# Moving ten of sixteen blocks of S5 angles and sines to the MLA head, and the other six into gate units 2 to 4

## The reference, cut to what matters

```
q_dn, kv_dn, k_rope, gate = jnp.split(h @ w_in, MLA_SPLITS, axis=-1)
q   = _rmsnorm(q_dn, q_norm) @ w_uq        # per head: 128 + 64
out = (v * jax.nn.silu(gate)) @ w_out
```

```
lam_dt  = lam * dt[:, None]
lam_bar = jnp.exp(lam_dt)
powers  = jnp.exp(lam_dt[None] * jnp.arange(1, S5_CHUNK + 1)[:, None, None])
xs      = associative_scan(combine, (a, bu)) + powers[None] * h[:, None]
```

## Time and profile before

| what | value |
|---|---|
| median of 3 runs | 1923.38 us (1921.63 to 1929.44) |
| the profiled execution, its own time | 1926.24 us |
| its span in the trace | 1924.3 us |
| mean granted TensorE clock | 0.945 |
| PE matmul busy | 1676.7 us, 87% |
| DVE, ACT, POOL busy | 635.7, 443.5 and 511.9 us |

### The profile page before, as it was taken

How to read it: one execution, slowest core, us unless ns; L and a number is a source line. 1 busy time by engine, 2 the same in 40 slices (tenths; PEclk the granted TensorE clock), 3 DMA queues, 4 the chain that set the end, 5 groups by cost and what they waited for, 6 DMA issues and landing times.

```text
span 1924.3 us, 27570 instructions
## 1 busy us (share of the span) xinstructions
PE 1676.7 (87%) x10824; PEld 1256.0 (65%) x10824; DVE 635.7 (33%) x1201; ACT 443.5 (23%) x986; POOL 511.9 (27%) x451
## 2 busy tenths in 40 slices
PE   3899599999999789996666679999989988999997
PEld 3444255555544478885555568888878876888886
DVE  4538655555610222305555510000122022233301
ACT  1413433332300110114445420000020101144300
POOL 0039999999999810000000000000000000000000
PEclk9999799999999889997888789999999999999999
DMA  8665525434544212264667644444334332344431
GB/s 268 183 186 197 213 77 166 153 131 140 174 149 164 109 44 66 88 231 149 210 210 218 194 147 153 153 153 153 131 109 131 120 100 88 110 153 153 148 121 60
DMA packets 225439, 283.69 MB, mean 147 GB/s; under 512 B 22498, under 2 KB 209477, under 8 KB 216901
## 3 DMA queue, kind: packets, MB, share of 16 engines
q1 hardware_dynamic: 214976, 231.78, 37.9%
q0 software_dynamic: 7040, 41.95, 6.2%
q10 hardware_dynamic: 3333, 8.71, 1.1%
HBM read 226.82 MB, written 47.19 MB: 142 GB/s over the span
## 4 chain that ended last, share of the span: by engine, by line
PE 72%; SPq 9%; DVE 8%; ACT 4%; DMA 3%; issue 3%; DVEq 0%; ACTq 0%; PEldq 0%
PE bank L814 34%; PE bank L1140 12%; SPq L640 9%; PE bank L1010 6%; PE bank L879 2%; DMA arena<-arena 2%; PE bank L838 2%; PE bank L1196 1%; PE bank L943 1%; PE bank L912 1%; PE bank L911 1%; PE bank L909 1%; PE bank L910 1%; PE bank L907 1%; ACT arena L1506 1%
## 5 line engine op out<-in xcount | busy, mean ns | idle before, releaser
L814 PE MATMUL bank<-ht,ring 128*128 128x256 f32 (+1 forms) x1664 | 421.9, 417 | 18.6 <-DVE ht L2113 9.0
L814 PEld LDWEIGHTS bank<-ht,ring 128*128 128x128 f32 x1664 | 319.6, 192 | 119.4 <-issue 80.6
L1140 PE MATMUL bank<-arena,ring 128*128 128x256 f32 x1024 | 222.8, 381 | 1.1 <-PEq L1131 1.1
L1140 PEld LDWEIGHTS bank<-arena,ring 128*128 128x128 f32 x1024 | 195.6, 191 | 28.0 <-issue 1.2
L814 PE MATMUL bank<-gate,ring 128*128 128x256 f32 (+1 forms) x640 | 194.8, 467 | 4.5 <-DVE gate L2166 3.4
L814 PEld LDWEIGHTS bank<-gate,ring 128*128 128x128 f32 x640 | 122.4, 192 | 76.5 <-issue 62.7
L1010 PE MATMUL bank<-ring,ht 128*128 128x256 f32 x512 | 113.6, 384 | 12.1 <-DVE ht L1783 12.1
L1010 PEld LDWEIGHTS bank<-ring,ht 128*128 128x128 f32 x512 | 98.2, 193 | 26.1 <-issue 12.7
L814 PE MATMUL bank<-arena,ring 128*128 128x256 f32 x480 | 107.8, 388 | 3.9 <-DVE arena L2228 3.9
L814 PEld LDWEIGHTS bank<-arena,ring 128*128 128x128 f32 x480 | 93.8, 196 | 17.7 <-DVE arena L2228 4.3
L2085 DVE SCALAR_TENSOR_TENSOR gate<-bank,col,gate 128x256 f32<-128x256 f32 x16 | 7.7, 481 | 197.1 <-ACT gate L1566 197.1
(11 more groups left out here) (355 smaller groups left out, 2342.5 us busy)
## 6 DMA issues: line engine op xcount, KB each, us to landing
ring<-in_s_w_glu SPq DMA_DIRECT2D x32, 1024.0 KB, 5.3
ring<-in_w_mod SPq DMA_DIRECT2D x24, 1024.0 KB, 7.9
ring<-in_w_up SPq DMA_DIRECT2D x22, 1024.0 KB, 5.1
s_b_powers<-arena POOLq DMA_DIRECT2D x16, 1024.0 KB, 4.3
s_c_powers<-arena POOLq DMA_DIRECT2D x16, 1024.0 KB, 4.9
ring<-in_s_w_in SPq DMA_DIRECT2D x16, 1024.0 KB, 5.3
arena<-s_b_powers SPq DMA_DIRECT2D x16, 1024.0 KB, 11.0
ring<-s_c_powers SPq DMA_DIRECT2D x10, 1024.0 KB, 7.6
```

Source lines behind the costliest of these rows:

```text
L814: mm = pe.matmul(psum[2 * (u % 2) + m][:, 0:mv.free_size()], ring[:, sl, k, m * P:(m + 1) * P], mv, start=(kg == 0 and k == 0), stop=(kg = ...
L1140: mm = pe.matmul(psum[4 * par + 2 * (s // 2) + m][:, 0:S], ring[:, sl, k, m * P:(m + 1) * P], yt[:, kg * 8 + k, :], start=(kg == 0 and k = ...
```

## The change

Blocks 0 to 9 move ahead. On DVE, angles 0 to 9 stand right behind the powers of `lam_bar`, ahead of the head's PSUM copies. On ACT, `trig` 0 to 9 stand behind the modulation of the input, ahead of the squares of the head. Since these blocks now use their memory before `ccol` is written, ACT waits before `b_and_c` until all ten stores have landed. Blocks 10 to 15 keep the wait for `bc_spilled` and stand on DVE ahead of the norms; on ACT they follow gate units 2, 3 and 4, two to a unit. PE, GpSimd and SP have the same instructions in the same order as before.

```
 ACT
             modulate(0)
+            for b in range(10):
+                trig(b)
             for j in range(2):
                 act.wait_ge(qkv_copied, j + 1)
                 act.activation(sq1[:, j, :], qd[:, j, :], ACT.Square).then_inc(sq_set, 1)
             act.wait_ge(qkv_copied, 3)
             act.activation(sq1[:, 2, :], kvd, ACT.Square).then_inc(sq_set, 1)
+            for par in range(2):
+                act.wait_ge(trig_stored[par], 16 * 5)
             b_and_c()
...
-            trigs = ((), (), (0, 1, 2), (3, 4, 5), (6, 7, 8, 9), (10, 11, 12, 13), (14, 15), ())
+            trigs = ((), (), (10, 11), (12, 13), (14, 15), (), (), ())
 DVE
+            for b in range(10):
+                angles(b)
             dve.wait_ge(par_got, 6)
             at = ring_at["mla_head"]
             dve.wait_ge(slot_done, at + 1)
...
             dve.wait_ge(bc_spilled, 8 * 16)
-            for b in range(6):
+            for b in range(10, NB5):
                 angles(b)
             dve.wait_ge(root_set, 2)
...
             tt(kr_rot, kr_rot, rot_t, ALU.add).then_inc(normed, 1)
-            for b in range(6, NB5):
-                angles(b)
```

More of the change, by code:

```diff
@@ L1329, in _ @@
             modulate(0)
[L1331 to L1342, removed]
             def trig(b):
@@ L1355, in trig, with gate_silu @@
                 act.dma_start(spill_trig[b], trig_out[par].rearrange("p z d q c -> p (z d q c)")).then_inc(trig_stored[par], 16)
-            trigs = ((), (), (0, 1, 2), (3, 4, 5), (6, 7, 8, 9), (10, 11, 12, 13), (14, 15), ())
+            for b in range(10):
+                trig(b)
+            for j in range(2):
+                act.wait_ge(qkv_copied, j + 1)
+                act.activation(sq1[:, j, :], qd[:, j, :], ACT.Square).then_inc(sq_set, 1)
+            act.wait_ge(qkv_copied, 3)
+            act.activation(sq1[:, 2, :], kvd, ACT.Square).then_inc(sq_set, 1)
+            for par in range(2):
+                act.wait_ge(trig_stored[par], 16 * 5)
+            b_and_c()
+            at, u0 = ring_at["mla_gate"], unit_at["mla_gate"]
+            def gate_silu(s):
+                act.wait_ge(slot_done, at + s + 1)
+                for m in range(2):
+                    act.activation(gate[:, 2 * s + m, :], psum[2 * ((u0 + s) % 2) + m][:, :], ACT.Silu)\
+                        .then_inc(unit_free[(u0 + s) % 2], 1)
+            trigs = ((), (), (10, 11), (12, 13), (14, 15), (), (), ())
             for s in range(8):
@@ L1825, in _, with angles @@
                 dve.tensor_copy(pw[:, z, :, GP5:P], pn[:, z, ::-1, GP5:P]).then_inc(par_got, 1)
+            def angles(b):
+                par = b % 2
+                if b >= 2:
+                    dve.wait_ge(trig_set, 2 * b - 2)
+                ph = phi[:, :].rearrange("p (d q) -> p d q", d=2)[:, :, b * BLK:(b + 1) * BLK].unsqueeze(3).to_broadcast(wide)
+                link(tt(trig_angle[par], ph, iota.unsqueeze(1).unsqueeze(1).to_broadcast(wide), ALU.mult))
+                link(ts(trig_near, trig_angle[par], MAGIC, None, ALU.add))
+                stt(out=trig_angle[par], in0=trig_near, scalar=-MAGIC, in1=trig_angle[par], op0=ALU.add, op1=ALU.subtract)\
+                    .then_inc(ang_set, 1)
+                dve.wait_ge(ang_set, b + 1)
+            for b in range(10):
+                angles(b)
             dve.wait_ge(par_got, 6)
```

## The result

| | before | after |
|---|---|---|
| median of 22 timed runs each | 1923.9 us (1918.05 to 1929.68) | 1928.54 us (1925.2 to 1933.75) |
| profiled execution, own time | 1926.24 us | 1928.11 us |
| its span | 1924.3 us | 1926.3 us |
| its mean granted clock | 0.945 | 0.941 |

The ratio after to before is 1.0024, with a 95% interval of 1.0014 to 1.0033. The change costs 4.6 us where I had forecast a gain of 1.6. That is within the 0.5% that I called no difference and inside the stated range, but it lies on the other side, and with these many runs the interval leaves out 1.

The account below looks back on a forecast made before the run. PE carries 72% of the chain, so its standstills and clock bound the kernel. Removed 26.8 less added 16.8 gives 10.0 us; less 8.4 lost beside GpSimd, 1.6 us faster: 1921.8 us, range 1912 to 1931.

Parts of the forecast that it names:

- +10.0: Ahead of the attention: 26.8 us removed less 16.8 us added, so attention and later layer norm come 10.0 us earlier.
- The stops go away: PE's stops before gate unit 7 and the attention vanish, but for 1.3 us of idle time.
- They are worth 28.1 us: PE's two stops with their clock losses: 8.05 + 1.7 + 15.30 + 3.05 = 28.1 us, the most to be won there.
- The first projection gives 3.05 us: Start of the attention: the first projection keeps its clock, taking 3.60 us instead of 6.65.
- Ten stores set the head back by 15.1 us: Head: `b_and_c` waits for ten stores and begins at 97.4 us, 15.1 later; bounds 9.6 and 25.5 later.
- The transposes at half clock cost 1.7 us: Before the gate: PE idles, its clock falls to 0.50 for the first transposes, costing 1.7 us (ends 0 and 3.05).
- Blocks 10 to 15 are free: Gate units 3 to 5: two blocks fit in each unit of 13.8 us, so they cost nothing.
- GpSimd ends at 676.6: GpSimd's power tables: start 15.1 us later, 6.6 us of contention come back, last table done at 676.6 instead of 668.1.
- The ten instructions lose 0.84 us each: Layer norm after the MLA layer: ten DVE instructions beside GpSimd lose 0.84 us each, 8.4 us in all.
- B: Layer norm: eight modulating instructions without waits keep GpSimd out, contention costs some 1 us, 9.0 won, 1914.4 us; chance 0.27.
- D: GpSimd's tables end near 668 us, only half of the ten instructions contend, about 4 us lost, 1917; chance 0.10.
- C: Head: stores land late, 5.8 us each, `b_and_c` 25.5 us later, 1932.2 us; decides from 16.7 us setback; chance 0.13.

Follow-up runs that it names:

- e5: The kernel before, run again unchanged for a second whole profile; 1925.68 us, ratio 1.0005.
- e3: The kernel after, with four output tiles instead of two for the head's ten blocks, and no wait for stores ahead of `b_and_c`; 1922.99 us, ratio 0.9984.
- e9: The kernel before, unchanged, a single execution; 1918.85 us.
- e10: The kernel before, unchanged, a single execution; 1917.52 us.
- e1: The kernel after, without GpSimd's 24 products of the last power-table block (its stores stay); 1918.5 us, ratio 0.9972.
- e7: The kernel of e6, with five of the eight DVE instructions that modulate the latents given to ACT; 1902.79 us, ratio 0.9884.
- e6: The kernel after, with no block in the head: blocks 0 to 5 run in gate units 0 and 1 with their own tiles; 1908.12 us, ratio 0.9914.
- e4: The kernel after, run again unchanged for a second profile; 1929.92 us, ratio 1.0024.

## Why the prediction was wrong

Four traces of each kernel give this account, against the prediction's own terms:

| term | predicted | measured | difference |
|---|---|---|---|
| start of the gate later | 16.8 | 113.6 - 94.6 = 19.0 | -2.2 |
| stops and clock, gate to attention | 28.1 - 1.3 - 3.05 = 23.75 | 22.5 | -1.25 |
| attention to reciprocal, the first projection's clock | 3.05 | 0.7 | -2.35 |
| reciprocal earlier | 10.0 | 4.2 | -5.8 |
| loss beside GpSimd, to the start of S5 | 8.4 | 7.8 | +0.6 |
| S5 starts | 1.6 earlier | 3.5 later | -5.1 |

The measured 22.5 is (231.9 - 94.6) - (228.4 - 113.6), and 7.8 is (680.7 - 661.1) - (677.2 - 665.3), both from unrounded means. Behind it the first 128 matmuls of L1010 take 30.63 to 30.82 us in the traces of after, 30.73 in the mean, and 29.34 to 30.63 in those of before, 29.84 in the mean: 0.9 us more. The clock stood at 0.50 for 5.8 us of it in the mean of after and for 4.0 in that of before, which is these 0.9 us. The prediction has no term for this, though it priced the same effect at PE's two stops. 3.5 + 0.9 = 4.4 us, beside the 4.6 us between the medians. Behind that point the traces show no difference between the kernels that is larger than their own scatter of some 5 us.

**The step that failed** is "+10.0" in the sum. Its mechanism was right, both of its terms were mis-sized: what the change removes was 22.5 + 0.7 = 23.2 us and not 26.8, what it adds ahead of the gate 19.0 and not 16.8, so that the reciprocal comes 4.2 us earlier and not 10.0. Of the 6.2 us between forecast and result 5.8 are here. Point by point:

- *The stops go away.* Right: no idle time before units 6 and 7, a rest of 1.22 us (1.3 forecast), the first projection in 3.70 us (3.6), the attention at 227.30 (226 to 227).
- *They are worth 28.1 us.* Too much. That was read from one execution, whose own time stood 2.9 us above the median. With the store of block 13 in time the long stop is 12 us and not 15. I noticed the 2.9 us, and corrected the total by it instead of asking which row held them.
- *The first projection gives 3.05 us.* It took 6.01 us in the mean of the traces of before and takes 3.70 now, 2.3 saved, and of this only 0.7 is still there at the reciprocal. 0.7 us goes at PE's first wait for DVE in the attention (L935), which is 1.27 us in the trace of after and 0.55 in that of before; where the last 0.9 goes the traces do not say. (The 4 us after which the clock fell were read at one stop and are no constant: ahead of the S5 layer it fell 2.3 us after PE's last matmul in the trace of before, and 5.4 in e5.)
- *Ten stores set the head back by 15.1 us.* 17.7 in the profile of after, 99.92 where 97.4 was forecast, and 19.0 in the mean. The first store landed after 7.6 us and not 5.8, that of block 4 after 6.1 and not 3.2; a pair of blocks without a late store took 4.72 us, less than my 5.2, and set by ACT. The last store was so issued at 97.20 and not at 94.1, and 2.6 us later, at 99.8, it landed; the squares were done under it, as forecast. The late ones were issued at 67.7, 70.0, 82.0 and 84.8 us, while loads of weights kept the DMA engines at a share of 0.8 or more; the other six landed within 2.6 to 3.1 us. The prediction had allowed for the first of these two stretches alone. e3 confirms the mechanism: without these waits the setback is 9.7 us.
- *The transposes at half clock cost 1.7 us.* They cost nothing. From the first copy of L1324 to the gate it is 12.62 us, and was 12.60. The kernel after in windows (length, then busy time of PE, PEld, DVE, ACT and POOL, then the granted clock):

```profile
85.00:86.00 1.00, 0.00 (x0) 0.00 (x0) 0.95 (x2) 0.00 (x0) 0.00 (x0) 0.50 0.93 313
...
104.00:106.00 2.00, 1.99 (x14) 1.78 (x13) 0.00 (x0) 2.00 (x4) 0.00 (x0) 0.75 0.00 0
106.00:108.00 2.00, 1.35 (x13) 1.08 (x11) 0.84 (x1) 2.00 (x4) 0.00 (x0) 1.00 0.00 0
```

  The clock did fall to 0.50, and was back before the gate. But ACT's copies set the pace in this stretch (8 of them 7.14 us after, 7.10 before), so PE's slowness lay under them. It was luck that this term of 1.7 us, which did not exist, stood for a part of the 3.9 us (19.0 - 15.1) that the stores and blocks cost beyond the forecast.
- *Blocks 10 to 15 are free.* Right, the row from 170.55 has no gap.
- *GpSimd ends at 676.6.* It ended later: its last store is issued at 682.46. I let 6.6 us of lost contention come back; with `b_and_c` 17.66 us later and the end 14.34 later it was 3.3. Most of what is missing was lost in the meeting itself: the two products of GpSimd beside DVE's long ones took 2.21 and 3.03 us instead of 1.10, 3.0 us together. It did not matter, since the ten instructions were over at 678.7.
- *The ten instructions lose 0.84 us each.* Right in the sum: 8.4 forecast, 7.8 measured, 9.89 us for the eight where I had 9.5. The 7.8 is measured against a before that in e9 and e10 already loses 1.7 and 0.4 us; against the 11.3 us from reciprocal to S5 without any meeting (e1, e5) the kernel after loses 8.3. It is not spread evenly. In the profile of after the two products lose 0.28 and 0.90 us, the eight 0.89 each. By the Trainium skill's rule (SBUF — State Buffer, "SBUF: two separate sides") each instruction waits for the holder of the shared port pair; the trace agrees, with 1.24 us per instruction beside products of 1.10 to 1.27 us on GpSimd, and so does e1, where GpSimd is at rest and DVE's rows are those of the kernel before (2.29 and 2.80 us).

Of the rivals, B is refuted by the 9.89 us, and D by 682.46: GpSimd was not near its end. C came about in part: stores landed late, and the setback was 19.0 us in the mean. I had given it 0.13, because I took a long landing for one case among many; but ten stores in a row make a chain in which a single long one is enough. It is not the whole account. C's mark "from a setback of 16.7 us on" stood beside 1.7 us for the clock, which fell away, so the mark was 18.4, and 19.0 is only 0.6 us beyond it. The other 3.6 us of the miss ahead of the norm (26.8 - 23.2) lie in what was removed: 1.25 us in the stops, 2.35 in the first projection's clock, in part because the one trace read had the long stops. No rival named this.

## What to carry to other kernels

Work that is moved off one idle stretch of PE must land where something covers it: in the head ten blocks cost 19 us, 9.3 of them waits for their stores, while in the gate units stores that landed later still, with an ACT wait of 6.59 us, cost nothing. A gain ahead of a point where DVE and GpSimd meet is lost there as long as GpSimd's end does not move with it, so look for what runs on GpSimd at the next stretch where DVE is on the chain, and give that work to ACT (e7). When a single profile is above the median of its kernel, ask which of its waits is long by chance before counting it as a gain.

## What the runs showed that I had not expected

- Eight DVE instructions of 0.35 us that follow each other without a wait do not hold GpSimd off. They took 1.24 us each (singly from 1.16 to 1.50, all eight) in every trace of after (9.89, 9.91, 9.90, 9.89 us), in e3 (9.90) and e6 (9.74). GpSimd does not suffer from these: its products beside them took 1.10 to 1.27 us, as without DVE, and only beside the two long products of DVE did single ones take 2.21 and 3.03.
- A granted clock of 0.50 costs nothing where ACT sets PE's pace (12.62 against 12.60 us).
- The same 512 KB store landed in 2.6 us at the least and up to 10.4, in one kernel, by what else was moving. One such store makes some 3.5 us of difference between the stops of an unchanged kernel (15.38 and 11.91 us).
- In all four traces of after the granted clock dips between 742 and 750 us (0.66, 0.84, 0.83 and 0.92 in the mean of 742 to 746), though what runs there is the same. Of the four traces of before it dips only in e9 (0.66 from 738 to 742). At the second place that e4 was to look at, it dips in all four of after (0.57 to 0.78 in the mean of 808 to 812), but also in three of the four of before (down to 0.60 between 800 and 812). Whether the first dip belongs to the change stays open; from the first matmuls' end to the end of the program the two kernels differ by 0.9 us in the mean, within the scatter.
